# Softmax division as diagonal matrices: two attention stages of a long one-core kernel

## The chip, the cores and the metric

The kernel runs on one core of a Trainium2 chip. One launch computes two transformer blocks of two layers each, all in 32-bit floats. The metric is the time of one execution on the device, in microseconds (us). The kernel before has run three times: 2238.98, 2239.80 and 2239.84 us, median 2239.8 us.

The engines are named as in the profile: PE is the matmul engine (TensorE), PEld its loading of stationary operands (weights), DVE the vector engine, ACT the scalar engine, POOL GpSimd, and SP the queue that issues most DMAs.

## The reference, cut to what matters

Two places of the reference are touched. The first is the dilated window attention of the first block (16 heads, 256 tokens, three dilation groups whose softmax is joint):

```python
p = jnp.exp(s - mx[..., None])
den = jnp.sum(p, axis=-1)
num = jnp.einsum('bdnqhk,bdnkhe->bdnqhe', p, vb.astype(jnp.float32))
...
o = (num / den[..., None]).astype(h.dtype).reshape(B, S, D_MODEL)   # after the groups are joined
```

The second is the differential attention in both layers of the second block (4 heads, two score maps for each head):

```python
p = jax.nn.softmax(jnp.where(mask, s, -jnp.inf), axis=-1)
a = p[:, :, 0] - lam * p[:, :, 1]
return jnp.einsum('bhqk,bkhe->bqhe', a.astype(v.dtype), v)
```

The rest (projections, norms, a convolution mixer, two squared-ReLU MLPs, retention, gated linear attention, routing and 32 experts for each layer) is the same before and after.

## The kernel before, in words

The order on each engine is written out by hand, and semaphores tie the engines together. Weights of about 2 MB a slab pass through a ring of six slots; SP loads a slab when PE has reported a slot free.

**Stage A, the dilated attention** (64 to 344 us of the profile). A loop over c = 0..7 handles two heads at a time. In each round PE makes six projections (`project`, line 1997) of the round's heads and, between them, the attention of the round before. An attention unit is one (head, half of the queries), u = 0..3; u and u+1 make a pair, so there are 16 pairs in all. For each unit:

- PE computes the scores (line 2020), DVE adds the mask and takes the maximum (line 1314), ACT computes the exponential into `att_s`, 128 queries by 512 keys, and its row sum (line 758).
- DVE takes the reciprocal of the sum (line 1323) and multiplies `att_s` by it in place, 128x512 (`scale_prob`, line 1324), and signals `prob_scaled`.
- PE turns `att_s` in four pieces of 128x128 with `te.transpose` against the identity matrix (`turn_p`, line 2030), so that keys lie on the partitions. ACT copies the result out of PSUM (line 766), and one projection later PE multiplies with the values (line 2040).

A pair's eight transposes stand together on PE, after a projection, in the first half of a round and in the second. In the last round the place of the projections is taken by parts of the output product (line 2050).

**Stage D, the differential attention** (around 1018 to 1053 us in layer 0, 1674 to 1709 us in layer 1). Eight units u = (head, half of the queries) for each layer, again in pairs. For each unit ACT makes two exponentials of 128x256, one for each map (line 859). DVE (`d_join`, lines 1503 to 1506) takes two reciprocals, scales map 0 in place, folds lambda into the second reciprocal (a 128x1 operation) and adds the scaled map 1 onto map 0. PE then turns the one joined map, two pieces of 128x128 (`d_turn`, line 2265). The pairs (0,1), (2,3), (4,5) and (6,7) stand between projections (lines 2156, 2163), scores (2253), values (2274) and the retention's products (2284, 2295, 2304).

`spread` (line 1910) is a helper that the prediction compares with: an ordinary matmul of 128x128 with `ones` as the stationary and a diagonal matrix as the moving operand. The diagonal is made by DVE at line 1147 as identity times a column of scalars. `spread` writes two matmuls for each call. `piece` of the experts (line 2493) is compared with too; it writes 16 ordinary matmuls with 128 moving columns for each call.

Of the kernel before, what the change touches and what calls it, by code (L numbers as in the profile page):

```python
# [31 lines left out]
P = 128  # L32
# [174 lines left out]
def program(nc, x_d, xp_d, common_d, const_a_d, const_2_d, param_1_d, param_2_d, param_r_d, pos_d,  # L207
# [8 lines left out]
    def sem(name):  # L216
        return enter(nc.semaphore(name))
# [50 lines left out]
    att_t = [take(512).rearrange("p (j q) -> p j q", j=4) for _ in range(2)]  # L268
    turn_a = take(NT * 6 * 16).rearrange("p (r h d) -> p r h d", r=NT, h=6)
# [68 lines left out]
    qd_n = tok_d.rearrange("p (i r n) -> p i r n", i=2, r=NT)  # L338
    gate_t, r_square, r_root = [tok_d[:, 512 * n:512 * n + 512] for n in (1, 2, 3)]
# [68 lines left out]
    def chunks(b, n):  # L408
# [27 lines left out]
    scored, masked, max_ready, prob_ready, prob_scaled, prob_turned, prob_copied, pv_done, o_copied = [  # L436
        sem("a_" + n) for n in (
            "scored", "masked", "max_ready", "prob_ready", "prob_scaled", "prob_turned", "prob_copied",
# [13 lines left out]
    d_gained, d_summed, d_ready, d_side, d_sided, d_scored, d_max, d_exp, d_joined, d_turned, d_copied, d_out = [  # L452
        sem("d_" + n) for n in ("gained", "summed", "ready", "side", "sided", "scored", "max", "exp", "joined",
# [614 lines left out]
    def _(dve):  # L1068
# [197 lines left out]
        if first:  # L1266
# [53 lines left out]
            def scale_prob(c, u):  # L1320
                p = u % 2
                dve.wait_ge(prob_ready, 4 * c + u + 1)
                own.step(ve.reciprocal(small[:, 6 + p:7 + p], small[:, 4 + p:5 + p]))
                ve.tensor_scalar(att_s[p], att_s[p], small[:, 6 + p:7 + p], None, ALU.mult
                                 ).then_inc(prob_scaled, 1)
            dve.wait_ge(const_a_in, 16)
            for c in range(KD + 1):
                for w in range(2):
                    if c < KD:
                        gain_q(c, 2 * w)  # L1330
                        gain_q(c, 2 * w + 1)
                    if c > 0:
                        mask(c - 1, 2 * w)
                        mask(c - 1, 2 * w + 1)
                    if c < KD:
                        root_q(c, w)
                    if c > 0:
                        scale_prob(c - 1, 2 * w)
                        scale_prob(c - 1, 2 * w + 1)
                    if c < KD:  # L1340
                        norm_q(c, w)
# [58 lines left out]
        if second:  # L1400
# [14 lines left out]
            for lay in range(DEPTH):  # L1415
# [84 lines left out]
                def d_join(u):  # L1500
# [3 lines left out]
                    own.inc(ve.tensor_scalar(att_d[p][:, 0, :], att_d[p][:, 0, :], small[:, 40:41], None, ALU.mult))  # L1504
                    own.step(ve.tensor_scalar(small[:, 42:43], small[:, 41:42], small[:, 28:29], None, ALU.mult))
                    ve.scalar_tensor_tensor(out=att_d[p][:, 0, :], in0=att_d[p][:, 1, :], scalar=small[:, 42:43],
                                            in1=att_d[p][:, 0, :], op0=ALU.mult, op1=ALU.add).then_inc(d_joined, 1)
# [61 lines left out]
                d_join(0)  # L1569
                d_join(1)  # L1570
# [3 lines left out]
                d_join(2)  # L1574
                d_join(3)
                d_mask(4)
                d_mask(5)
                d_join(4)
                d_join(5)
# [3 lines left out]
                d_join(6)  # L1583
                d_join(7)
# [292 lines left out]
    def _(pe):  # L1877
# [106 lines left out]
        if first:  # L1984
# [39 lines left out]
            def turn_p(c, u):  # L2024
                n = 4 * c + u
                pe.wait_ge(prob_scaled, n + 1)
                if n >= 2:
                    pe.wait_ge(prob_copied, n - 1)
                for j in range(4):
                    e = te.transpose(bank(3 + u % 2)[:, P * j:P * j + P], att_s[u % 2][:, P * j:P * j + P], com("ident"))  # L2030
# [96 lines left out]
        if second:  # L2127
# [12 lines left out]
            for lay in range(DEPTH):  # L2140
# [117 lines left out]
                def d_turn(u):  # L2258
                    pe.wait_ge(d_joined, lay * 8 + (u + 1))
# [472 lines left out]
```

## Time and profile before

| | |
|---|---|
| median of three runs | 2239.8 us |
| the profiled execution, its own time | 2239.8 us |
| its span, first to last instruction | 2238.0 us |
| PE busy | 2136.5 us, 95% of the span |
| PEld busy | 1348.7 us, 60% |
| DVE busy | 876.9 us, 39% |
| ACT busy | 343.1 us, 15% |
| chain of waits, by engine | PE 76%, DMA 19%, DVE 2%, issue 1%, ACT 1% |

The times of all instructions come from one execution, read by the hardware profiler. Matmuls are pipelined: the profile gives each a duration of its own that reaches over the next one's start, so what a run of matmuls costs is read from the distance between starts in the timeline, not from the mean duration. The two columns that end a line of a group are the busy time with the mean of one, and the idle time of the engine just before the group with what ended it.

### The profile page before, as it was taken

Reading aid. Unit: us, or ns where it says so; the run is one execution under the profiler, and the core shown is the slowest. Engines: PE = TensorE matmul, PEld = TensorE weight load, DVE = VectorE, ACT = ScalarE, POOL = GpSimd, SP = SyncE. Lnnn points to the kernel's source line nnn. Section 1 sums busy time; section 2 is a strip of 40 time slices with the busy share of each in tenths; the row PEclk is TensorE's granted clock in tenths of the full one; section 3 lists DMA queues with packets and bytes.
Section 4 is the critical chain, followed back from the end, with each engine's and each line's share of the span. In section 5 each row is a group of like instructions: output and inputs, shape, how many; then the busy total and the mean of one; then the engine's idle time right before and its main releaser. Section 6 shows DMA issues by size and latency. Waiting matters only on the chain.

```text
span 2238.0 us, 25518 instructions
## 1 busy us (share of the span) xinstructions
PE 2136.5 (95%) x10046; PEld 1348.7 (60%) x10046; DVE 876.9 (39%) x1937; ACT 343.1 (15%) x657; POOL 21.5 (1%) x28
## 2 busy tenths in 40 slices
PE   9999999999999999999999989888999999889888
PEld 5666668888888888757644443343657554333333
DVE  3444433455331455465443222222355643222222
ACT  1222221000000000224111101010323111100110
POOL 0000000000000000000000000000000000000000
PEclk9999999999999999999999999999999999999999
DMA  7333346787445686423399999999632599999996
GB/s 312 113 130 125 132 151 241 264 303 267 142 151 221 254 309 246 143 102 132 157 369 411 429 429 428 429 428 417 236 122 76 229 401 421 428 429 428 429 428 279
DMA packets 108582, 623.22 MB, mean 278 GB/s; under 512 B 6096, under 2 KB 8528, under 8 KB 73424
## 3 DMA queue, kind: packets, MB, share of 16 engines
q1 hardware_dynamic: 94816, 566.63, 63.0%
q0 software_dynamic: 12672, 50.33, 6.1%
q10 hardware_dynamic: 1008, 5.07, 0.6%
q8 instruction: 59, 0.97, 0.2%
q14 instruction: 27, 0.22, 0.0%
HBM read 620.96 MB, written 1.05 MB: 278 GB/s over the span
## 4 chain that ended last, share of the span: by engine, by line
PE 76%; DMA 19%; DVE 2%; issue 1%; ACT 1%; SPq 0%; DVEq 0%; ACTq 0%
DMA ring<-in_w_up 18%; PE ps L1922 15%; PE ps L2480 14%; PE ps L1997 11%; PE ps L1959 10%; PE ps L2163 5%; PE ps L2514 4%; PE ps L2156 3%; PE ps L2313 2%; PE ps L2452 2%; PE ps L2493 1%; PE ps L2050 1%; PE ps L2020 1%; PE ps L2040 1%; PE ps L2030 1%
## 5 line engine op out<-in xcount | busy, mean ns | idle before, releaser
L2480 PE MATMUL ps<-ring,hT 128*64 128x512 f32 x1984 | 460.8, 619 | 67.9 <-DMA ring<-in_w_up 52.5
L2480 PEld LDWEIGHTS ps<-ring,hT 128*64 128x64 f32 x1984 | 166.7, 142 | 352.1 <-issue 345.6
L1922 PE MATMUL ps<-hT,ring 128*128 128x256 f32 x1408 | 309.8, 381 | 3.6 <-ACT tmp L690 2.4
L1922 PEld LDWEIGHTS ps<-hT,ring 128*128 128x128 f32 x1408 | 267.9, 191 | 41.9 <-issue 3.1
L1997 PE MATMUL ps<-ring,hT 128*128 128x384 f32 x768 | 256.4, 487 | 1.9 <-DMA ring<-in_a_wqkv 1.8
L2514 PE MATMUL ps<-ring,arena 128*64 128x512 f32 x1024 | 226.8, 595 | 1.4 <-ACT arena L995 1.4
L1959 PE MATMUL ps<-arena,ring 128*128 128x256 f32 x1024 | 224.5, 378 | 0.0
L1959 PEld LDWEIGHTS ps<-arena,ring 128*128 128x128 f32 x1024 | 193.3, 189 | 28.1
L1997 PEld LDWEIGHTS ps<-ring,hT 128*128 128x128 f32 x768 | 142.2, 190 | 93.2 <-DMA ring<-in_a_wqkv 2.5
L2514 PEld LDWEIGHTS ps<-ring,arena 128*64 128x64 f32 x1024 | 70.6, 137 | 139.8 <-issue 138.0
L1219 DVE SCALAR_TENSOR_TENSOR arena<-arena,small 128x512 f32<-128x512 f32 x168 | 126.4, 752 | 6.0
L2452 PE MATMUL ps<-arena 128*128 128x256 f32 x512 | 124.0, 385 | 2.0 <-DVE arena L1751 2.0
L2452 PEld LDWEIGHTS ps<-arena 128*128 128x128 f32 x512 | 91.9, 189 | 36.9 <-issue 26.4
L2163 PE MATMUL ps<-ring,hT 128*128 128x512 f32 (+1 forms) x320 | 113.9, 511 | 0.0
L1733 DVE RECIPROCAL arena<-arena 128x512 f32<-128x512 f32 x32 | 107.3, 3354 | 1.1
L1732 DVE TENSOR_SCALAR arena<-arena 128x512 f32<-128x512 f32 x32 | 13.7, 429 | 220.1 <-ACT arena L988 220.1
L1738 DVE TENSOR_TENSOR arena<-arena,ps 128x512 f32<-128x512 f32 x32 | 34.5, 1080 | 145.4 <-PE ps L2480 145.4
L1751 DVE COPY arena<-ps 128x512 f32<-128x512 f32 x32 | 22.2, 692 | 170.0 <-PE ps L2514 170.0
L2163 PEld LDWEIGHTS ps<-ring,hT 128*128 128x128 f32 x320 | 59.5, 190 | 46.4 <-issue 42.5
L1212 DVE TENSOR_TENSOR arena<-tmp 128x1024 f32<-128x1024 f32 x16 | 19.6, 1227 | 169.9 <-ACT tmp L690 169.9
L983 ACT ACTIVATE hT<-arena 128x512 f32 x60 | 38.1, 636 | 272.3 <-PE ps L2480 261.6
L1286 DVE TENSOR_TENSOR arena<-ps,arena 128x384 f32<-128x384 f32 x32 | 17.8, 556 | 144.7 <-ACT arena L738 144.7
(380 smaller groups left out, 1756.6 us busy)
## 6 DMA issues: line engine op xcount, KB each, us to landing
ring<-in_w_gate SPq DMA_DIRECT2D x44, 2048.0 KB, 17.1
ring<-in_w_up SPq DMA_DIRECT2D x44, 2048.0 KB, 17.3
ring<-in_w_down SPq DMA_DIRECT2D x44, 2048.0 KB, 15.9
ring<-in_mlp_w SPq DMA_DIRECT2D x32, 2048.0 KB, 8.0
arena<-in_w_mod POOLq DMA_DIRECT2D x24, 2048.0 KB, 9.7
ring<-in_w_up SPq DMA_DIRECT2D x40, 1024.0 KB, 9.0
ring<-in_w_down SPq DMA_DIRECT2D x40, 1024.0 KB, 8.9
ring<-in_a_wqkv SPq DMA_DIRECT2D x24, 1536.0 KB, 6.8
```

What stands on the lines that cost most here:

```text
L983: e = sc.activation(xg.rearrange("p (k s) -> p k s", k=KD)[:, :, SB * m:SB * m + SB], src, ACT.Copy)
L1219: e = ve.scalar_tensor_tensor(out=mod_acc, in0=w[:, k, :], scalar=small[:, 16 + k:17 + k], in1=mod_acc, op0=ALU.mult, op1=ALU.add)
L1733: own.step(ve.reciprocal(eb, eb))
L1922: e = te.matmul(out[:, j, :], w[:, k, c0 + 128 * j:c0 + 128 * j + 128], src[:, k, :], start=(k == order[0]), stop=(k == order[-1]))
L1959: e = te.matmul(chunks(0, 8)[:, o, :], w[:, k, 128 * o:128 * o + 128], u3[j % 3][:, k, :], start=(start and k == 0 and o % 2 == 0), stop=F ...
L1997: e = te.matmul(bank(r)[:, 0:WIDTH_A], h3[:, k, r * P:(r + 1) * P], weights[:, k, :], start=(k == HEAD_ORDER[0]), stop=(k == HEAD_ORDER[-1]))
L2156: e = te.matmul(out[:, j, :], w[:, k, c0 + P * j:c0 + P * j + P], h3[:, k, :], start=(k == SUM_ORDER[0]), stop=(k == SUM_ORDER[-1]))
L2163: e = te.matmul(out, h3[:, k, r * P:(r + 1) * P], w[:, k, c0:c0 + width], start=(k == 0), stop=(k == KD - 1))
L2313: e = te.matmul(out_2(o), w[:, k, P * (o % 4):P * (o % 4) + P], src, start=(start and k == ks[0] and o % 2 == 0), stop=False, skip_group_c ...
L2452: e = te.matmul(chunks(0, 8)[:, k, :], ysb[:, k * P:(k + 1) * P], selT, start=False, stop=False, skip_group_check=True)
L2480: e = te.matmul(bank(b)[SB * h:SB * h + SB], xg[:, P * k + SB * h:P * k + SB * h + SB], slabs.tile(n + h).rearrange("p (k n) -> p k n", k= ...
L2514: e = te.matmul(bank(6 + o)[SB * h:SB * h + SB], ueT[:, P * k + SB * h:P * k + SB * h + SB], slabs.tile(n + h).rearrange("p (k n) -> p k n ...
```

## The change: what it does

Both stages no longer divide the probabilities on DVE. Instead DVE makes a 128x128 diagonal matrix (the identity times a column of scalars) for each divisor, and PE multiplies the undivided probabilities with that matrix, in place of the transpose. For a block X of queries by keys and a diagonal D, the matmul with X stationary and D moving gives the transposed X with each query's column scaled.

- Stage A: `scale_prob` becomes `diagonal`; the 128x512 operation becomes one of 128x128. `turn_p` keeps four instructions for each unit, now `te.matmul` with `den_diag`.
- Stage D: `d_join` becomes `d_diagonal`: a 128x128 diagonal for map 0, and one for map 1 that holds minus lambda over its sum. `d_turn` issues four matmuls for each unit where two transposes stood: the two maps are added in PSUM (`start` on map 0, `stop` on map 1).
- Two new 128x128 tiles hold the diagonals of stage A; those of stage D lie in `tok_d`. Two semaphores are renamed. No wait is added or taken away.

```diff
-            def scale_prob(c, u):
+            def diagonal(c, u):
                 p = u % 2
                 dve.wait_ge(prob_ready, 4 * c + u + 1)
                 own.step(ve.reciprocal(small[:, 6 + p:7 + p], small[:, 4 + p:5 + p]))
-                ve.tensor_scalar(att_s[p], att_s[p], small[:, 6 + p:7 + p], None, ALU.mult
-                                 ).then_inc(prob_scaled, 1)
+                ve.tensor_scalar(den_diag[p], com("ident"), small[:, 6 + p:7 + p], None, ALU.mult
+                                 ).then_inc(diag_ready, 1)
...
-                def d_join(u):
+                def d_diagonal(u):
                     p = u % 2
                     dve.wait_ge(d_exp, lay * 8 + (u + 1))
                     own.step(ve.reciprocal(small[:, 40:42], small[:, 36 + 2 * p:38 + 2 * p]))
-                    own.inc(ve.tensor_scalar(att_d[p][:, 0, :], att_d[p][:, 0, :], small[:, 40:41], None, ALU.mult))
+                    own.inc(ve.tensor_scalar(den_d[2 * p], com("ident"), small[:, 40:41], None, ALU.mult))
                     own.step(ve.tensor_scalar(small[:, 42:43], small[:, 41:42], small[:, 28:29], None, ALU.mult))
-                    ve.scalar_tensor_tensor(out=att_d[p][:, 0, :], in0=att_d[p][:, 1, :], scalar=small[:, 42:43],
-                                            in1=att_d[p][:, 0, :], op0=ALU.mult, op1=ALU.add).then_inc(d_joined, 1)
+                    ve.tensor_scalar(den_d[2 * p + 1], com("ident"), small[:, 42:43], None, ALU.mult
+                                     ).then_inc(d_diag, 1)
...
             def turn_p(c, u):
...
                 for j in range(4):
-                    e = te.transpose(bank(3 + u % 2)[:, P * j:P * j + P], att_s[u % 2][:, P * j:P * j + P], com("ident"))
+                    e = te.matmul(bank(3 + u % 2)[:, P * j:P * j + P], att_s[u % 2][:, P * j:P * j + P],
+                                  den_diag[u % 2], start=True, stop=True)
...
                 def d_turn(u):
...
                     for k in range(NT):
-                        e = te.transpose(bank((2, 7)[u % 2])[:, k * P:(k + 1) * P], att_d[u % 2][:, 0, k * P:(k + 1) * P],
-                                         com("ident"))
+                        for w in range(2):
+                            e = te.matmul(bank((2, 7)[u % 2])[:, k * P:(k + 1) * P], att_d[u % 2][:, w, k * P:(k + 1) * P],
+                                          den_d[2 * (u % 2) + w], start=(w == 0), stop=(w == 1))
                     e.then_inc(d_turned, 1)
```

In stage A the order on PE stays as it was. Before, around the first pair of a round (x8 counts the instructions that the code writes):

```order
L1997 MATMUL ps<-ring,hT 128x384 x8
L2030 MATMUL ps<-common,arena 128x128 x8
L1997 MATMUL ps<-ring,hT 128x384 x8
L2040 MATMUL ps<-arena 64x128 x8
L2020 MATMUL ps<-arena 128x256 x2
```

The same place now, with the changed kernel's line numbers (`project` is 1999, `turn_p` 2032):

```order
L1999 MATMUL ps<-ring,hT 128x384 x8
L2032 MATMUL ps<-arena 128x128 x8
L1999 MATMUL ps<-ring,hT 128x384 x8
L2043 MATMUL ps<-arena 64x128 x8
L2022 MATMUL ps<-arena 128x256 x2
```

Nothing moved; the eight instructions of a pair read the diagonal (in `arena`) where they read the identity (in `common`).

In stage D, PE from the scores of head 2 on, before (2265 is `d_turn`):

```order
L2253 MATMUL ps<-arena 128x256 x4
L2163 MATMUL ps<-ring,hT 128x256 x8
L2265 MATMUL ps<-common,arena 128x128 x4
L2253 MATMUL ps<-arena 128x256 x4
L2163 MATMUL ps<-ring,hT 128x256 x8
L2274 MATMUL ps<-arena 128x256 x2
```

The same place now (2269 is `d_turn`):

```order
L2256 MATMUL ps<-arena 128x256 x4
L2166 MATMUL ps<-ring,hT 128x256 x8
L2269 MATMUL ps<-arena 128x128 x8
L2256 MATMUL ps<-arena 128x256 x4
L2166 MATMUL ps<-ring,hT 128x256 x8
L2278 MATMUL ps<-arena 128x256 x2
```

A pair has eight written instructions where it had four; their place among the others is the same.

## Rows read from the trace of the kernel before

**Rows 1.** Windows view: stretch, busy by engine (instructions), PE clock, DMA share, GB/s.
```profile
64.00:344.00 280.00, 279.33 (x1350) 179.48 (x1350) 122.02 (x424) 78.11 (x176) 0.00 (x0) 1.00 0.35 126
```

**Rows 2.** Chain of waits, 64 to 344 us, shares by line.
```profile
by line: PE ps L1997 73.0%; PE ps L2040 5.9%; PE ps L2020 5.8%; PE ps L2050 5.8%; PE ps L2030 5.3%; PE ps L2007 4.1%; ACT arena L751 0.2%; issue 0.1%
```

**Rows 3.** Timeline, PE, stage A, two pairs: start us, length us, instructions.
```profile
104.58 1.19 PE L2030 MATMUL ps<-common,arena 128*128 128x128 f32 x8
105.60 5.33 PE L1997 MATMUL ps<-ring,hT 128*128 128x384 f32 x16
...
118.50 1.04 PE L2030 MATMUL ps<-common,arena 128*128 128x128 f32 x8
119.38 0.49 PE L2007 MATMUL ps<-common,arena 128*128 128x128 f32 x3
```

**Rows 4.** Timeline, PE, `spread` called twice.
```profile
613.06 0.61 PE L1910 MATMUL ps<-rstd,common 128*128 128x128 f32 x4
613.50 0.61 PE L1910 MATMUL ps<-arena,common 128*128 128x128 f32 x4
613.95 2.32 PE L1922 MATMUL ps<-hT,ring 128*128 128x256 f32 x10
```

**Rows 5.** Timeline, PE, one call of `piece` and what follows.
```profile
1123.82 3.84 PE L2493 MATMUL ps<-tmp,arena 128*128 128x128 f32 x32
1127.49 0.60 PE L2501 MATMUL ps<-common,arena 128*128 128x128 f32 x4
```

**Rows 6.** Waits view, stage A, weight loads: us in total, times, longest us.
```profile
PEld ps L2030 <- DVE arena L1324: 3.6, 13, 0.4
```

**Rows 7.** Groups by form, DVE: count, busy us, mean ns, idle before.
```profile
L1324 DVE TENSOR_SCALAR arena<-arena,small 128x512 f32<-128x512 f32 x32 | 15.6, 487 | 1.1
L1147 DVE TENSOR_SCALAR rstd<-common,tok 128x128 f32<-128x128 f32 x10 | 2.4, 283 | 0.2
L1504 DVE TENSOR_SCALAR arena<-arena,small 128x256 f32<-128x256 f32 x16 | 5.7, 355 | 0.6
```

**Rows 8.** Timeline, PE, stage D of layer 0, three of its four pairs.
```profile
1028.04 0.60 PE L2265 MATMUL ps<-common,arena 128*128 128x128 f32 x4
1028.57 1.13 PE L2253 MATMUL ps<-arena 64*128 64x256 f32 x8
...
1039.96 3.72 PE L2163 MATMUL ps<-ring,hT 128*128 128x256 f32 x16
1043.78 0.44 PE L2265 MATMUL ps<-common,arena 128*128 128x128 f32 x2
1044.90 0.44 PE L2265 MATMUL ps<-common,arena 128*128 128x128 f32 x2 [0.68 <-DVE arena L1506]
1045.27 1.14 PE L2253 MATMUL ps<-arena 64*128 64x256 f32 x8
1046.33 3.72 PE L2163 MATMUL ps<-ring,hT 128*128 128x256 f32 x16
1049.89 1.03 PE L2274 MATMUL ps<-arena 128*128 128x256 f32 x4
...
1051.92 0.66 PE L2265 MATMUL ps<-common,arena 128*128 128x128 f32 x4
1052.41 1.03 PE L2274 MATMUL ps<-arena 128*128 128x256 f32 x4
```

**Rows 9.** Timeline, DVE, unit 5 of layer 0: the join.
```profile
1044.36 0.48 DVE L1506 SCALAR_TENSOR_TENSOR arena<-arena,small 128x256 f32<-128x256 f32 x1
```

**Rows 10.** Timeline, ACT, the end of unit 5's exponential.
```profile
1043.43 0.19 ACT L859 ACTIVATION_READ_ACCUMULATOR arena<-arena,small 128x1 f32 x1
```

**Rows 11.** Timeline, PEld, the output product after stage D, layer 0.
```profile
1065.26 6.77 PEld L2313 LDWEIGHTS ps<-hT,ring 128*128 128x128 f32 x32 [1.43 <-DVE hT L1478]
```

**Rows 12.** Windows view, start of the experts of layer 0 (columns as above).
```profile
1110.00:1120.00 10.00, 10.00 (x48) 3.38 (x50) 7.65 (x22) 0.60 (x1) 0.00 (x0) 1.00 0.14 57
1140.00:1200.00 60.00, 60.00 (x314) 28.86 (x312) 20.57 (x41) 9.35 (x19) 0.00 (x0) 1.00 0.99 409
```

More of the change, by code:

```diff
@@ L268, in program @@
     att_t = [take(512).rearrange("p (j q) -> p j q", j=4) for _ in range(2)]
+    den_diag = [take(P) for _ in range(2)]
     turn_a = take(NT * 6 * 16).rearrange("p (r h d) -> p r h d", r=NT, h=6)
@@ L338, in program @@
     qd_n = tok_d.rearrange("p (i r n) -> p i r n", i=2, r=NT)
+    den_d = [tok_d[:, P * n:P * n + P] for n in range(4)]
     gate_t, r_square, r_root = [tok_d[:, 512 * n:512 * n + 512] for n in (1, 2, 3)]
@@ L435, in program @@
         "half_done", "unit_read", "q_gained", "q_summed", "q_ready", "q_turned", "q_copied")]
-    scored, masked, max_ready, prob_ready, prob_scaled, prob_turned, prob_copied, pv_done, o_copied = [
+    scored, masked, max_ready, prob_ready, diag_ready, prob_turned, prob_copied, pv_done, o_copied = [
         sem("a_" + n) for n in (
-            "scored", "masked", "max_ready", "prob_ready", "prob_scaled", "prob_turned", "prob_copied",
+            "scored", "masked", "max_ready", "prob_ready", "diag_ready", "prob_turned", "prob_copied",
             "pv_done", "o_copied")]
@@ L451, in program @@
         "product", "ready", "scored", "decayed", "used")]
-    d_gained, d_summed, d_ready, d_side, d_sided, d_scored, d_max, d_exp, d_joined, d_turned, d_copied, d_out = [
-        sem("d_" + n) for n in ("gained", "summed", "ready", "side", "sided", "scored", "max", "exp", "joined",
+    d_gained, d_summed, d_ready, d_side, d_sided, d_scored, d_max, d_exp, d_diag, d_turned, d_copied, d_out = [
+        sem("d_" + n) for n in ("gained", "summed", "ready", "side", "sided", "scored", "max", "exp", "diag",
                                 "turned", "copied", "out")]
@@ L1337, in _ @@
                     if c > 0:
-                        scale_prob(c - 1, 2 * w)
-                        scale_prob(c - 1, 2 * w + 1)
+                        diagonal(c - 1, 2 * w)
+                        diagonal(c - 1, 2 * w + 1)
                     if c < KD:
@@ L1568, in _ @@
                 dve.wait_ge(d_sided, lay * 4 + 4)
-                d_join(0)
-                d_join(1)
+                d_diagonal(0)
+                d_diagonal(1)
                 d_mask(2)
@@ L1573, in _ @@
                 rope_r(0)
-                d_join(2)
-                d_join(3)
+                d_diagonal(2)
+                d_diagonal(3)
                 d_mask(4)
                 d_mask(5)
-                d_join(4)
-                d_join(5)
+                d_diagonal(4)
+                d_diagonal(5)
                 rope_r(1)
@@ L1582, in _ @@
                 d_mask(7)
-                d_join(6)
-                d_join(7)
+                d_diagonal(6)
+                d_diagonal(7)
                 decayed(0)
@@ L2025, in turn_p @@
                 n = 4 * c + u
-                pe.wait_ge(prob_scaled, n + 1)
+                pe.wait_ge(diag_ready, n + 1)
                 if n >= 2:
@@ L2258, in d_turn @@
                 def d_turn(u):
-                    pe.wait_ge(d_joined, lay * 8 + (u + 1))
+                    pe.wait_ge(d_diag, lay * 8 + (u + 1))
                     if u >= 2:
```

## The prediction

> **What bounds the kernel now.** I read the windows view of stage A first. PE is busy 279.33 of 280.00 us at a granted clock of 1.00, the upper of its two levels, while DVE has 122 us of work and ACT 78 [rows 1]. The chain of waits says the same: every step of the stretch but 0.3% is a PE line, and the turned probabilities (line 2030) are 5.3% of it [rows 2]. So in stage A a nanosecond on PE is a nanosecond of the kernel, and DVE time is worth only what PE waits for it. The waits view gives that: the weight loads of line 2030 wait 3.6 us in all for DVE's line 1324, 13 times [rows 6], most of it under matmuls that still run. What reaches the matmuls is seen in the timeline, from the start of a pair to the next group's start. In the second half of a round a pair takes 119.38 - 118.50 = 0.88 us; in the first half 105.60 - 104.58 = 1.02 us [rows 3]. The pair without a stall is 8 transposes at 0.109 to 0.110 us. The other loses 0.14 us between its two units, because DVE scales the second block too late. Seven rounds have such a first half; the eighth, under the output product, I take to be without the stall.
>
> **What one instruction costs.** The change swaps a transpose for an ordinary matmul of the same shape, 128x128 stationary and 128 moving columns, 32-bit. The number of instructions in the code does not settle this; the number of recorded ones does. A pair of stage A writes 8 transposes and the timeline has x8 [rows 3]. `spread`, the same kind of matmul as the new one (a diagonal made by DVE is moving), writes 2 for each call and the timeline has x4 [rows 4]. `piece` writes 16 and has x32 [rows 5]. So each ordinary 32-bit matmul goes through PE twice and a transpose once. One pass costs (613.95 - 613.06) / 8 = 0.111 us [rows 4] and, with a restart in it, (1127.49 - 1123.82) / 32 = 0.115 us [rows 5]. I take 0.112 us a pass: an ordinary matmul is 0.224 us, against 0.109 for the transpose. The first distance after PE has stood still is longer: 3.67 - 31 x 0.1115 = 0.21 us for `piece` [rows 5], about 0.10 more than a pass.
>
> The Trainium skill, page "TensorE: Matmul & The Clock Gate", section Terms, speaks harder against this change: the transpose mode of trn2 is four times faster for FP32. The trace has 0.224 to 0.109, a ratio of 2.05, so the page's ratio does not hold for these rows; what it would give stands with the third rival.
>
> **Stage A, PE.** 32 units in 16 pairs. A pair was 8 records and becomes 8 matmuls, 16 records: 16 x 0.112 = 1.79 us. The nine pairs without a stall gain 1.79 - 0.88 = 0.91 us each, 8.2 us. The seven with a stall gain 1.79 - 1.02 = 0.77 us each, 5.4 us, since the stall goes: PE needs the second unit only after 8 passes of the first, 0.90 us later instead of 0.44, and DVE has it earlier too. Sum 13.6 us, all of it on the path.
>
> **Stage A, DVE.** Line 1324 goes from 487 ns (128x512) to a 128x128 multiplication of the identity, 283 ns in line 1147 [rows 7]: 32 x 0.204 = 6.5 us less. None of it counts beyond the 7 x 0.14 = 1.0 us of stall that the sum above already takes away. ACT's copy of a turned unit starts up to 0.91 us later, but a whole projection of 5.3 us lies between it and the matmul that reads it [rows 3]. No DVE or ACT step comes late by this.
>
> **Stage D, PE.** For each unit 2 transposes become 4 matmuls, 8 records; a pair goes from 4 records to 16.
>
> - Pair (0,1): now 1028.57 - 1028.04 = 0.53 us, of which 4 x 0.109 = 0.44 are passes and 0.09 is the change to the next group's shape, which stays [rows 8]. After: 1.79 + 0.09 = 1.88 us, so +1.35 us. Pair (2,3) has the same four records and the same +1.35.
> - Pair (6,7): now 1052.41 - 1051.92 = 0.49 us [rows 8], with a short restart. After: 1.79 + 0.10 = 1.89 us, so +1.40 us.
> - Pair (4,5) is the one place where DVE covers the work. The projection of 16 ahead of it would let go at 1039.96 + (1049.89 - 1046.33) = 1043.52, but unit 4 starts at 1043.78 and unit 5 at 1044.90, after an idle 0.68, and the next group at 1045.27 [rows 8]. On DVE the two big operations of a unit go from 355 and 486 ns (line 1504 and the join) to 283 each [rows 7, 9], 0.27 us less. Unit 4 is then ready at about 1043.51, just when PE is. Its 8 passes with a restart need 8 x 0.112 + 0.10 = 1.00 us, to 1044.52. Unit 5 cannot begin its reciprocal before its exponential ends at 1043.62 [rows 10]; the join ended at 1044.84 [rows 9], and of the 0.27 us the exponential leaves some 0.23. It is ready at 1044.61, and PE starts it at about 1044.66. Its 8 passes, a restart and the change of shape take 0.90 + 0.10 + 0.09, to 1045.75. That is +0.48 us, with 0.9 us of the work in the old waits. Were nothing covered it would be +1.35 us, were all of it covered 0.
>
> A layer gains 1.35 + 1.35 + 0.48 + 1.40 = 4.58 us, two layers 9.2 us. DVE loses 16 x 0.27 = 4.4 us of work in stage D, worth nothing beyond pair (4,5).
>
> **Does it arrive at the end?** After stage D the norms wait for the values that PE makes, and PE waits 1.43 us for them at 1065.26 [rows 11]: that chain starts with PE's last values, so it moves with them. The experts later are bound by weights: the DMA engines are 0.99 busy from 1140 to 1200 us. But from 1110 to 1120 they are at 0.14 [rows 12]: the slots are full and the stream restarts only when PE frees one. A late PE therefore starts the stream late by the same amount, and nothing is absorbed. The granted clock is 1.00 already [rows 1, 12], so nothing is to be won or lost there.
>
> **Sum.** 13.6 + 9.2 = +22.8 us on the profiled execution's own 2239.8 us, which is also the median of the runs shown: 2262.6 us, 1.0% slower.
>
> **Rivals.**
>
> 1. The second record isn't a second pass for this matmul, so that it costs 0.112 us. For: the code of stage A has as many instructions as before. Then stage A is 9 x (0.90 - 0.88) + 7 x (0.90 - 1.02) = -0.7 us; in stage D a pair has 8 records, 0.90 us: +0.46, +0.46, +0.51, and pair (4,5) about +0.04, so 1.5 a layer. In all +2.3 us: 2242.1 us, no change that can be told. Against it stand x4 for two and x32 for sixteen [rows 4, 5]. Chance 3%.
> 2. The other side: PE has room, and the DVE work is what counts. The place is the wait ahead of a pair, the price of a pair on PE is 0.91 us, and DVE decides only where PE now waits longer than that. If it did everywhere, the 6.5 + 4.4 us of DVE would come back: 2228.9 us, faster. Only pair (4,5), with 1.0 us of waiting, passes that point; stage A's 0.14 us does not [rows 3, 8]. Chance 1%.
> 3. Each new pass shows its weight load: its stationary block changes every time and only 128 columns cover it, so that a pass costs the restart's 0.21 us. Stage A: a pair 3.41 us, 7 x 2.39 + 9 x 2.53 = 39.5 us; stage D 3.0 + 3.0 + 3.0 + 1.8 = 10.7 a layer. In all +61 us: 2300.7 us. Against it: `piece` changes its stationary block each time too, and 32 records need 3.67 us [rows 5]. Chance 3%. The skill's factor of four makes a matmul 0.436 us, a pair of stage A 3.49 us and a sum of +62.9 us, 2302.7 us; it would come out here, and this 3% is for both.
> 4. The experts' stream absorbs what stage D adds, because it is the bound there [rows 12]; stage A's part stays: 2239.8 + 13.6 = 2253.4 us. Against it the 0.14 of DMA share before it. Chance 5%.
>
> **How the numbers follow.** The forecast has 88%. Its own range is 2259 to 2266: below, a pass of 0.110 instead of 0.112 takes 384 x 0.002 = 0.8 us off and a better cover in pair (4,5) up to 1.0; above, 0.115 adds 1.2 us, pairs (4,5) without cover 1.7, and the two together with small new waits some 3.4. The runs shown lie within 0.9 us of each other. To hold 8 in 10 with some of the fourth rival I give 2257 to 2268. What a measurement here can tell from no change is about 0.2%, 4.5 us: slower by more holds the forecast and rivals 3 and 4, 96%; within it rival 1, 3%; faster rival 2, 1%.
>
> **What would show it.** In the changed profile: x256 records of `turn_p` and x128 of `d_turn`; the distance from a pair's start to the next group 1.79 us in both halves of a round, the stall between units gone; DVE's diagonal at 283 ns; in stage D 1.9 us for three pairs and about 2.2 from PE's arrival for (4,5); the same DMA-bound stretch, moved by about 18 us in layer 0 and 23 in layer 1. I am wrong if the pairs have x8, if passes lie 0.2 us apart, or if the experts' stretch ends less late than it begins.

## The result, and the profile after

The changed kernel takes 2253.98 us, the median of four runs (2249.54 to 2255.23); the kernel before took 2239.82 us in four runs beside it (2238.98 to 2240.95). The ratio is 1.0064, with a 95% interval from 1.0053 to 1.0077: 14.3 us slower, 11.9 to 17.2. The prediction said slower, with 2262.6 us and a range down to 2257. The direction was right; the time lies 3 us below that range, and some 8 us of the forecast loss did not arrive.

The profiled execution of the changed kernel took 2256.0 us, its span 2254.2 us.

**Stage A** is where the time goes. The windows view over its 292.2 us (columns as in [rows 1]) shows the same full PE, and less DVE work:

```profile
69.80:362.00 292.20, 291.53 (x1472) 194.49 (x1472) 115.08 (x420) 80.25 (x175) 0.00 (x0) 1.00 0.33 120
```

The timeline of PE at the two pairs of [rows 3] (fences of this document leave rows out where `...` stands):

```profile
111.45 1.95 PE L2032 MATMUL ps<-arena 128*128 128x128 f32 x16
113.23 5.33 PE L1999 MATMUL ps<-ring,hT 128*128 128x384 f32 x16
...
126.14 1.95 PE L2032 MATMUL ps<-arena 128*128 128x128 f32 x16
127.92 0.49 PE L2009 MATMUL ps<-common,arena 128*128 128x128 f32 x3
```

A pair has x16 records where it had x8, and both halves of a round take the same 1.78 us (113.23 - 111.45, 127.92 - 126.14): the stall in the first is gone. The groups by form (`turn_p`, `d_turn` and the diagonal of stage A) and the waits view of the stage agree. Of the old 3.6 us of waiting [rows 6], 1.1 us in six waits are left:

```profile
L2032 PE MATMUL ps<-arena 128*128 128x128 f32 x256 | 31.2, 275 | 0.0
L2269 PE MATMUL ps<-arena 128*128 128x128 f32 x128 | 16.4, 279 | 0.0
L1326 DVE TENSOR_SCALAR arena<-common,small 128x128 f32<-128x128 f32 x32 | 9.2, 287 | 1.1
```
```profile
PEld ps L2032 <- DVE arena L1326: 1.1, 6, 0.2
```

**Stage D** of layer 0, PE, all four pairs; it answers to [rows 8]:

```profile
1045.14 1.94 PE L2269 MATMUL ps<-arena 128*128 128x128 f32 x16
1047.02 1.13 PE L2256 MATMUL ps<-arena 64*128 64x256 f32 x8
...
1055.95 1.94 PE L2269 MATMUL ps<-arena 128*128 128x128 f32 x16
1057.73 1.03 PE L2278 MATMUL ps<-arena 128*128 128x256 f32 x4
...
1063.32 2.28 PE L2269 MATMUL ps<-arena 128*128 128x128 f32 x16
1065.53 1.14 PE L2256 MATMUL ps<-arena 64*128 64x256 f32 x8
...
1072.18 2.05 PE L2269 MATMUL ps<-arena 128*128 128x128 f32 x16
1074.07 1.03 PE L2278 MATMUL ps<-arena 128*128 128x256 f32 x4
```

The distances from a pair to the next group are 1.88, 1.78, 2.21 and 1.89 us.

**Where it comes back.** The table sets the start of the same instruction in both traces against each other. A lasting change of the delay is time lost or won between two rows. (Delays are taken from unrounded times.)

| place on PE | before, us | after, us | delay |
|---|---|---|---|
| first `turn_q` (line 2007, now 2009) | 37.36 | 42.50 | 5.14 |
| last pair of stage A, group behind it | 339.36 | 358.11 | 18.74 |
| the sums after it | 389.31 | 406.39 | 17.08 |
| stage D, layer 0, behind the last pair | 1052.41 | 1074.07 | 21.65 |
| experts' loop, layer 0 | 1266.48 | 1287.18 | 20.70 |
| `permute` for layer 1 (line 2137, now 2140) | 1546.86 | 1564.70 | 17.83 |
| turns of the last expert pair | 1564.85 | 1581.35 | 16.50 |
| stage D, layer 1, behind the last pair | 1708.33 | 1729.39 | 21.06 |
| experts' loop, layer 1 | 1922.41 | 1942.49 | 20.08 |
| gates of the last expert pair (line 2480, now 2484) | 2203.02 | 2220.92 | 17.89 |
| end of the span | 2238.0 | 2254.2 | 16.2 |

Stage A adds 13.60 us, stage D 4.57 us in layer 0 (over 17.08) and 4.56 us in layer 1 (over 16.50). Then some 4 us go again at the end of each layer, at the one place where PE's program has an `If`. After the experts' loop stands `pe.If(more_blocks(pe) > 0)` for further blocks of routed tokens; here PE takes the `Else` and goes on with `permute`, or in layer 1 with the last expert pair. PE before, at that place in layer 0 and in layer 1 (a number in brackets is the idle time ahead of the group and what ended it):

```profile
1536.60 7.09 PE L2514 MATMUL ps<-ring,arena 128*64 128x512 f32 x32
1546.86 1.93 PE L2137 MATMUL ps<-arena 128*128 128x16 f32 x16 [3.18 <-issue]
...
2203.02 1.60 PE L2480 MATMUL ps<-ring,hT 128*64 128x512 f32 x6 [3.44 <-issue]
```

And after:

```profile
1557.27 7.09 PE L2518 MATMUL ps<-ring,arena 128*64 128x512 f32 x32
1564.70 1.93 PE L2140 MATMUL ps<-arena 128*128 128x16 f32 x16 [0.34 <-PE ps L2518]
...
2220.92 1.51 PE L2484 MATMUL ps<-ring,hT 128*64 128x512 f32 x6 [1.27 <-ACTq L1064]
```

"issue" means that nothing which the profile shows was waited for. The 3.18 us become 0.34, the 3.44 us 1.27: 2.84 and 2.17 us. The rest of the two fours is PE's clock. In before, the stretch shortly behind the gap runs at the lower of its two levels, 1.2 GHz; in after the same place runs at 2.4 GHz. (Such a stretch is called half-clock below; in the windows its PE clock is 0.50, or a value between where it fills a part.) Windows of before (the gap of layer 0, the stretch behind it, the stretch behind the gap of layer 1):

```profile
1543.70:1546.80 3.10, 0.00 (x0) 0.00 (x0) 0.85 (x2) 0.60 (x1) 0.00 (x0) 1.00 1.02 420
1549.00:1552.40 3.40, 2.77 (x8) 0.92 (x10) 0.48 (x2) 0.00 (x0) 0.00 (x0) 0.51 1.01 417
2204.30:2207.70 3.40, 3.40 (x10) 1.19 (x8) 0.00 (x0) 0.00 (x0) 0.00 (x0) 0.50 1.01 417
```

And of after, in layer 0 (2222.0 to 2225.4 us, in layer 1, has 1.00 too):

```profile
1567.40:1570.80 3.40, 3.34 (x16) 1.20 (x18) 0.00 (x0) 0.00 (x0) 0.00 (x0) 1.00 1.02 422
```

That takes another 1.33 us (17.83 to 16.50) and 1.69 us (17.89 to 16.20). In all 4.17 and 3.86 us, 8.0 us in these two profiles (the recorded expectations add the rounded parts and say 8.1).

The trace also has the branch instruction itself, on PE's sequencer (durations in ns, least, median and greatest of the two layers; then their starts). Before, and below it after:

```profile
L2581 PEldq COMPARE_BRANCH  x2: 5922/5993/6064, 1540.5 to 2196.2; - x2
```
```profile
L2585 PEldq COMPARE_BRANCH  x2: 333/340/347, 1561.2 to 2216.3; - x2
```

The sequencer reaches the branch while matmuls still wait ahead of PE. In before it stays in it for 5.9 and 6.1 us, so that the queued matmuls run out and PE stands still; in after it is through in a third of a microsecond.

What the branch waits for is PE's own code, as I read it. The profile lists instruction traffic as a queue of its own; the section on queues, before and then after (packets, MB, share):

```profile
q8 instruction: 59, 0.97, 0.2%
```
```profile
q8 instruction: 60, 0.98, 0.2%
```

0.97 MB in 59 packets is 16 KB a packet. In before such a packet begins at 1543.91, 0.8 us after the start of the last matmul of line 2514 (1543.10), and PE goes on 3 us later. In after the packet of this place begins at 1564.84, when `permute` has already started at 1564.70. The Trainium skill, page "Perfetto Trace Analysis", section "The 4-stage abstract model", says that an instruction has 64 bytes; a packet would then be 256 instructions, by my estimate from that figure. No row here shows an instruction's size, but the packet counts of the runs below agree with 256: 59 packets in the kernels with 0, 8 or 192 PE instructions more than before, 60 with 256 or 448, 62 with 768.

The change makes PE's code longer. In the records a written transpose is one record of a weight load and one of a matmul, two instructions; a written 32-bit matmul is twice that, four. Stage A's 128 written ones add 256 instructions, exactly one block; stage D adds 96 in a layer, 32 matmuls at four instead of 16 transposes at two. At the branch of layer 0 the whole change has moved the code by 352, at that of layer 1 by 448 (the trace of after has 448 more instructions, 25966 against 25518).

The remaining differences in the table belong to single executions: the 5.1 us at the start are half-clock stretches, discussed with `before_again`, and the 1.7 us after stage A are a stretch at 0.66 in before (374 to 379 us) that after has not. About 1 us goes in each layer between stage D and the experts' loop (21.65 to 20.70, 21.06 to 20.08), and I leave it open; in layer 0 it goes between 1189 and 1266 us, where the second profile of the same kernel shifts by 0.2 us against before and the other profiles by -1.6 to +1.8.

### The profile page after: what moved, and what is told of

Same layout as the page of the kernel before. It is cut to its first block, busy times and chain, and to the rows that moved or that the text cites. A ratio compares the mean times of both kernels' runs of the same rounds, so it can differ in the third digit from the quotient of the medians.

```text
span 2254.2 us, 25966 instructions
## 1 busy us (share of the span) xinstructions
PE 2160.2 (96%) x10270; PEld 1368.6 (61%) x10270; DVE 866.7 (38%) x1937; ACT 346.8 (15%) x657; POOL 21.5 (1%) x28
## 4 chain that ended last, share of the span: by engine, by line
PE 77%; DMA 19%; DVE 2%; ACT 1%; issue 1%; SPq 0%; DVEq 0%; ACTq 0%
DMA ring<-in_w_up 18%; PE ps L1924 15%; PE ps L2484 14%; PE ps L1999 11%; PE ps L1961 10%; PE ps L2166 5%; PE ps L2518 4%; PE ps L2159 3%; PE ps L2317 2%; PE ps L2456 2%; PE ps L2497 1%; PE ps L2032 1%; PE ps L2053 1%; PE ps L2022 1%; PE ps L2043 1%; PE ps L2269 1%
## 5 line engine op out<-in xcount | busy, mean ns | idle before, releaser
L2484 PEld LDWEIGHTS ps<-ring,hT 128*64 128x64 f32 x1984 | 157.6, 141 | 354.0 <-issue 349.9
```

The lines of the kernel that those rows point to most:

```text
L2484: e = te.matmul(bank(b)[SB * h:SB * h + SB], xg[:, P * k + SB * h:P * k + SB * h + SB], slabs.tile(n + h).rearrange("p (k n) -> p k n", k= ...
```

## The experiments

The landmarks in the traces serve as the measure; "delay" is always against the profile of before. The theory (theory 1 of the expectations): the local costs are as forecast, and some 8 us come back at the two branches because the code was moved. Its rivals: one of the two stages costs less than its distances say, or the experts' weight stream absorbs stage D's part.

**`a_only`: stage A's half of the change alone, `d_only`: stage D's.**

```diff
+    den_diag = [take(P) for _ in range(2)]
-                ve.tensor_scalar(att_s[p], att_s[p], small[:, 6 + p:7 + p], None, ALU.mult
+                ve.tensor_scalar(den_diag[p], com("ident"), small[:, 6 + p:7 + p], None, ALU.mult
-                    e = te.transpose(..., com("ident"))          # turn_p
+                    e = te.matmul(..., den_diag[u % 2], start=True, stop=True)
```

> Stage A's part of the change alone. Every theory agrees on the local cost: 16 pairs of 16 records, +13.6 us over stage A. They differ on what comes back later. Theory 1 (code place): PE's code after the experts' loop is read from memory in blocks of 16 KB, and whether PE stands still after the jump there depends on where the target lies in a block. The 128 additional records are 256 PE instructions, weight load and matmul, which at 64 bytes each is one whole block: the phase is that of the kernel before, so the gap of about 3.2 us before line 2137 stays and nothing is given back: about 2253 us. Theory 2 (the experts' weight stream absorbs what a stage adds before it): only stage D's share can be absorbed, so again about 2253. Theory 3 (PE's additional work in A is hidden somewhere): below 2249.

> Stage D's part of the change alone, +4.58 us in each layer before the experts. Theory 1 (code place): the target of the jump after the experts' loop moves by 96 instructions in layer 0 and by 192 in layer 1 within its 16 KB block, as in the whole change; the gap falls from 3.2 to about 0.3 us and the half-clock window that follows it goes, 4.2 us in layer 0 and some 3.9 in layer 1. With about 1 us a layer from the weight stream, 2239.8 + 9.2 - 8.1 - 1.9 = 2239.0 us, no change. Theory 2 (the stream absorbs): about 2239.8 to 2240, and then the delay against the kernel before is already gone while the experts' loop runs, not at its end. Theory 3 (nothing is given back): 2249.

`a_only` took 2253.04 us (2250.90 to 2257.18), ratio 1.0071 [1.0055, 1.0088]; `d_only` 2240.72 us (2238.16 to 2245.09), ratio 1.0006 [0.9996, 1.0016]; the kernel before in the same job 2239.36 us. Stage D's half costs nothing that can be told in sum, though each layer's stage D takes its 4.6 us. `permute` of layer 0 in `a_only`:

```profile
1558.12 3.18 PE L2139 MATMUL ps<-arena 128*128 128x16 f32 x16 [3.35 <-issue]
```

and in `d_only`:

```profile
1553.45 1.93 PE L2138 MATMUL ps<-arena 128*128 128x16 f32 x16 [0.34 <-PE ps L2516]
```

A whole block more in front of the branch leaves the gap; 96 instructions remove it, and in layer 1 the 192 of `d_only` leave 1.27 us instead of 3.44. In `a_only` stage A moves the delay from 1.19 to 14.79 us, 13.60 again. In `d_only` the delay is 9.26 us at the end of stage D and 9.37 us at 1514 us, deep in the weight-bound loop: the stream absorbs nothing in layer 0, and 2.5 us come back behind the loop there. In layer 1 about 3.9 us come back behind the loop and another 2.3 us inside it, where before has six half-clock stretches and `d_only` five.

**The gap and the clock come apart in these two profiles.** `d_only` has no gap in layer 0 and yet a half-clock stretch behind the branch; `a_only` has a gap of 3.34 us in layer 1 and none. Windows of `d_only`, then of `a_only`:

```profile
1557.40:1560.70 3.30, 3.30 (x10) 0.98 (x8) 0.00 (x0) 0.00 (x0) 0.00 (x0) 0.50 1.02 415
```
```profile
2216.00:2222.00 6.00, 6.00 (x30) 2.42 (x28) 0.00 (x0) 0.00 (x0) 0.00 (x0) 1.00 1.02 419
```

Over all thirteen profiles of this document (those of the kernels further below among them), nine have the gaps and four have none. The half-clock stretch behind the branch is there in 16 of the 18 places with a gap and in 2 of the 8 without. From the start of the loop's last group of line 2514 to the turns of the last expert pair, layer 0 takes 28.25 us in before and 29.8 to 30.1 in the other eight with gaps, against 24.08 or 25.77 us without; layer 1 takes 24.3 to 26.2 us against 22.24. The means differ by 4.9 and 3.5 us, 8.3 us in all. So 8 us is an average of two parts: 5 us or a little more of standstill, which every kernel with gaps has at both branches, and about 3 us of clock, which is more often there behind a gap but can come or stay away in a single execution.

**`phase`: the kernel before, its code moved by 96 and 192 instructions without stage A or D being touched.** The warm-up matmuls of `fill` are cut into more and narrower ones, with about the same number of columns.

```diff
-            fill(6, 3)
+            fill(30, 3, 83)                      # 30 of 83 columns for 6 of 416
-                fill(FILL, 4)                    # FILL = 8
+                fill(*((32, 4, 104) if lay else (FILL, 4)))
```

> The kernel before, with nothing of the change. The 6 warm-up matmuls of 416 columns at the start are 30 of 83, and in layer 1 the 8 warm-up matmuls of the routing are 32 of 104: the same columns, 96 PE instructions more by layer 0's jump and 192 by layer 1's. Theory 1: the gap after the experts' loop falls to about 0.3 us in both layers and the clock does not fall behind it: 2239.8 - 4.2 - 3.9 = about 2231.7 us, faster. Theory 2 and theory 3: nothing changes, 2239.8 us.

2236.89 us (2234.72 to 2238.25), ratio 0.9989 [0.9979, 0.9999]. Both gaps are gone, as expected (0.34 us in layer 0, 1.27 us in layer 1; the branch takes 0.35 and 0.33 us, and 4.2 and 3.9 us of delay go). The time missed, because narrow warm-ups are not as short as their columns. Start of the kernel before, and below it of `phase`, both at a granted clock of 1.00:

```profile
3.52 7.42 PE L1884 MATMUL ps<-common 128*128 128x416 f32 x12 [3.52 <-DMA param<-in_param]
...
12.73 3.49 PE L1997 MATMUL ps<-ring,hT 128*128 128x384 f32 x10 [1.78 <-DMA ring<-in_a_wqkv]
```
```profile
3.48 13.09 PE L1884 MATMUL ps<-common 128*128 128x83 f32 x60 [3.48 <-DMA param<-in_param]
16.37 2.06 PE L1997 MATMUL ps<-ring,hT 128*128 128x384 f32 x3
```

60 records take 12.89 us (16.37 - 3.48), 0.215 us for 83 columns, where 12 of 416 took 7.42 in all. The first projection starts 3.6 us late, and the narrower warm-ups of layer 1 cost 0.5 us: 8.0 - 4.1 = 3.9 us would be left, and 2.5 us (0.2 to 4.7) were measured.

**`after_back`: the changed kernel, its code moved on to whole blocks (512 and 768 instructions), so that the gaps should return.**

```diff
-            fill(6, 3)
+            fill(30, 3, 83)
-                fill(FILL, 4)
+                fill(*((48, 4, 69) if lay else (24, 4, 139)))
```

> The changed kernel with more and narrower warm-up matmuls (same columns), so that layer 0's jump lies 512 and layer 1's 768 PE instructions behind the kernel before, whole 16 KB blocks. Theory 1: the gap of 3.2 us is back in both layers, with the half-clock window: about 8 us slower than the changed kernel, near 2262. Theory 2 and 3: the same as the changed kernel, 2254.

2270.69 us (2270.32 to 2271.27), ratio to before 1.0145 [1.0128, 1.0162]. The gap is back (3.47 us in layer 0, 3.34 in layer 1). It overshot the expected time by the same fault as `phase`: its first projection starts at 16.40 us against 13.27 in after, 3.1 us, and the 48 warm-ups of 69 columns in layer 1 cost about 4.0 us: 2254.0 + 8.0 + 3.1 + 4.0 = 2269.1 us. These 96 records in its timeline:

```profile
1780.59 10.83 PE L1886 MATMUL ps<-common 128*128 128x69 f32 x96
1791.26 0.38 PE L2435 MATMUL ps<-arena 128*128 128x64 f32 x2
```

That is 0.111 us a record ((1791.26 - 1780.59) / 96), what 128 columns cost in [rows 4].

**`phase_skip`: 96 instructions more, but placed in the branch that PE does not take.**

```diff
                 with pe.If(more_blocks(pe) > 0):
+                    for _ in range(24):
+                        te.matmul(bank(4)[:, 0:1], zeros, com("ones")[:, 0:1], start=False, stop=False,
+                                  skip_group_check=True)
```

> The kernel before, with 24 matmuls of one column (96 PE instructions with their weight loads) put into the branch behind the experts' loop that these inputs don't take, in both layers. Nothing more is executed; layer 0's jump stays where it was and its target moves by 96 instructions, layer 1's jump by 96 and its target by 192. Theory 1a (only the target's place in its 16 KB block counts): both gaps fall as they did with the same targets, 2239.4 - 4.2 - 3.9 = about 2231.3 us. Theory 1b (the distance from the jump counts, what was fetched ahead): layer 0's gap stays 3.2 us, layer 1's may stay, 2235 to 2239.4. Theory 2 (code place has no part, the gain in the last such run was the warm-up's): 2239.4.

**`phase_2`: 96 and 192 instructions, added by warm-ups of 104 columns alone.**

```diff
-                fill(FILL, 4)
+                fill(4 * FILL, 4, 104)
```

> The kernel before, with the 8 warm-up matmuls of 416 columns of the routing as 32 of 104 in both layers, and the start as it was. Theory 1: targets 96 and 192 instructions later, gaps gone, -4.2 and -3.9 us, and +0.5 us a layer for the narrower warm-up as it showed in the last such run: 2239.4 - 8.1 + 1.0 = 2232.3 us. Theory 2: 2240.4.

The kernel before in this job took 2239.59 us. `phase_skip` took 2241.41 us (2235.77 to 2244.61), ratio 0.9999 [0.9987, 1.0010], and the gaps stay (3.41 and 3.37 us; the branches take 6.14 and 5.94); `phase_2` took 2231.64 us (2227.51 to 2238.39), ratio 0.9968 [0.9958, 0.9978]. `permute` of layer 0 in `phase_skip` (its first 8 records), then in `phase_2`:

```profile
1548.65 1.51 PE L2137 MATMUL ps<-arena 128*128 128x16 f32 x8 [3.41 <-issue]
```
```profile
1543.55 1.93 PE L2137 MATMUL ps<-arena 128*128 128x16 f32 x16 [0.34 <-PE ps L2514]
```

Both kernels move `permute` by the same number of instructions, and only one loses the gap. So it is not the place of the target in its block that decides, but where the loop and the branch ahead of it lie, or how far the target is from them. `phase_2` is faster than the kernel before and the changed one with nothing but narrower warm-ups: 8.0 us by the medians, 7.2 by the ratio (4.9 to 9.4). Its own profile gives 2.5 us at the branch of layer 0, where a half-clock stretch is left, and 3.9 in layer 1. That the medians come so near to the 8 us is in part luck, since the narrower warm-ups cost some 0.5 us a layer.

**`warm`: a rival for the delay at the start (the half-clock stretches come from PE's idle 1.78 us ahead of the first slab), and `before_again`: the kernel before once more.**

```diff
-            fill(6, 3)
+            fill(8, 3)
```

> The kernel before, with 8 instead of 6 warm-up matmuls at the start. The profiles so far differ by 0 to 7.5 us in when the first attention work is reached, by half-clock windows in the first 31 us. Theory S (PE's idle time before the first slab lets the clock fall): the idle 1.8 us goes, the windows in the first 31 us with it, about 2 us less in the median and a narrower spread. Rival (the windows come whatever PE does in that gap, or by chance in each execution): 2239.4, the same spread. The jump's targets move by 8 instructions only; the gap behind the experts' loop stays at about 3.2 us.

> The kernel before, word for word, for a second profile. If the half-clock windows at the start and at 375 us are a matter of the execution and not of the kernel, they lie elsewhere this time, and the first attention work starts up to 5 us later or not; the gap behind the experts' loop is 3.2 us again in layer 0 and 3.3 in layer 1.

(The expectation calls the rival that the idle time is the cause "theory S".) `warm` took 2238.90 us (2236.95 to 2244.55), ratio 0.9997 [0.9987, 1.0007]. The idle time goes, the first projection is where it was, and the half-clock stretch comes at 22.8 us all the same:

```profile
12.68 3.49 PE L1997 MATMUL ps<-ring,hT 128*128 128x384 f32 x10 [0.48 <-DMA ring<-in_a_wqkv]
```

`before_again` (one run, 2245.09 us) has no edit at all, and yet a half-clock stretch at the start that before did not have. Windows of `before_again` at 20 to 25 us, of after at 25 to 30; before has 1.00 from 20 to 30 us:

```profile
20.00:25.00 5.00, 5.00 (x18) 3.21 (x19) 1.95 (x12) 0.10 (x1) 0.00 (x0) 0.66 1.02 434
```
```profile
25.00:30.00 5.00, 5.00 (x9) 2.58 (x8) 2.15 (x10) 0.49 (x1) 0.00 (x0) 0.50 1.01 430
```

Its first `turn_q` comes 0.9 us late. Among the kernels whose PE code up to there is that of before, that delay is 0.9 (`phase_2`) to 5.1 us (after), and `a_only` has 1.2. The start is thus a matter of the execution; the 5.1 us of after's profile are no part of the change. The gaps at the branches are a matter of the kernel: `before_again` has them as before, 3.46 and 3.45 us.

**`after_whole`: the changed kernel on whole blocks (512 and 768) once more, with warm-ups of 104 columns or wider.**

```diff
-            fill(6, 3)
+            fill(12, 3, 208)
-                    fill(3, 7)                   # and the second fill(3, 7) likewise
+                    fill(9, 7, 139)
-                fill(2, 7)
+                fill(6, 7, 139)
-                fill(FILL, 4)
+                fill(4 * FILL, 4, 104)
```

> The changed kernel with its targets again a whole number of 16 KB blocks behind the kernel before (512 instructions in layer 0, 768 in layer 1), this time by warm-up matmuls of no fewer than 104 columns, since those of 69 and 83 cost about 4 us each time they ran. Theory 1: the gaps are back, +8.1 us on 2254.0, +1 us for the warm-ups: 2263, where the forecast of 2262.6 stood. If the forecast's two sums (13.6 and 9.2 us) were too large, it is nearer 2255.

2264.96 us (2263.52 to 2265.47) beside 2240.52 us, ratio 1.0105 [1.0078, 1.0132]. `permute` of layer 0 (its first 11 records):

```profile
1566.23 2.11 PE L2140 MATMUL ps<-arena 128*128 128x16 f32 x11 [3.25 <-issue]
```

With the gaps back in place the change costs about what was forecast: +24.4 us by the medians, 23.5 by the ratio (17.5 to 29.6), where the sum had +22.8 and the narrower warm-ups may bring about 1 us more (the estimate of the expectation).

**`a_ident` and `a_relief`: the two halves of stage A's change apart.** In `a_ident` PE multiplies with the identity and DVE scales as before; in `a_relief` DVE makes the diagonals and PE transposes as before, so that the division of stage A is left out.

```diff
-                    e = te.transpose(..., com("ident"))                                # a_ident
+                    e = te.matmul(..., com("ident"), start=True, stop=True)
-                ve.tensor_scalar(att_s[p], att_s[p], small[:, 6 + p:7 + p], ...)       # a_relief
+                ve.tensor_scalar(den_diag[p], com("ident"), small[:, 6 + p:7 + p], ...)
```

> The kernel before, with stage A's transposes as ordinary matmuls against the identity, and the division on DVE as it was: the cost of the second pass by itself. In stage A a pair takes 1.79 us in both halves of a round, without a stall between its units, +13.6 us from the first turned query to the end of the values, the same as with DVE relieved. If DVE's relief has a part in it, more. Its place in the code is a whole block later, so the gap behind the experts' loop stays.

> The kernel before, with DVE making the 128x128 diagonal in stage A and PE keeping its transposes: the division in stage A is left out. DVE's relief by itself: the seven pairs of 1.02 us take 0.88, -1.0 us over stage A, and nothing else.

One run each: 2253.27 and 2237.10 us. Over stage A the delay of `a_ident` goes from 1.76 to 15.59, +13.83 us; that of `a_relief` from 1.06 to 0.08, -0.98 us. A pair in the first half of a round in `a_ident`, then in `a_relief`:

```profile
108.06 1.99 PE L2030 MATMUL ps<-common,arena 128*128 128x128 f32 x16
109.89 1.46 PE L1997 MATMUL ps<-ring,hT 128*128 128x384 f32 x4
```
```profile
105.54 1.04 PE L2031 MATMUL ps<-common,arena 128*128 128x128 f32 x8
106.42 0.81 PE L1998 MATMUL ps<-ring,hT 128*128 128x384 f32 x2
```

The second passes are the whole price. DVE's relief is worth 1.0 us alone (a pair goes from 1.02 to 0.88 us). Beside them it is worth 0.2 us in these single profiles (13.83 against 13.60), since the longer first unit already covers most of the stall (1.83 against 1.78 us).

## Why the prediction was right in its steps and wrong in its sum

- **What one instruction costs: right.** x256 and x128 records, 1.78 us for 16 of them, 0.111 us a pass against 0.112. Rival 1 wanted x8 a pair, rival 3 distances of 0.2 us; neither is there.
- **Stage A: right.** 13.6 us forecast, 13.60 measured in the changed kernel and in `a_only`. The stall of seven pairs was there and went (`a_relief`: 0.98 us for 7 x 0.14).
- **Stage A, DVE: right.** 287 ns a diagonal (283 forecast), and nothing that DVE or ACT does comes late. Rival 2 fell with `a_relief`: taking the DVE work away gives 1 us, not 6.5.
- **Stage D: right.** 1.88, 1.78, 2.21 and 1.89 us a pair against 1.88, 1.88, about 2.2 and 1.89 (pair (2,3) is followed by another group than the forecast took, and was 0.10 us shorter before as well); 4.57 and 4.56 us a layer against 4.58. In pair (4,5) unit 5's reciprocal does wait for its exponential, as worked out:

```profile
1063.45 0.17 DVE L1505 RECIPROCAL small<-small 128x2 f32<-128x2 f32 x1 [0.20 <-ACT arena L861]
```

- **"Does it arrive at the end?": this step failed.** It asked of the norms, the experts' weight stream and the clock whether they would give time back, and found that none would. For the stream that was right (`d_only`, 9.26 to 9.37 us). But it took the rest of PE's program to be the same program, later. It is the same instructions at another place in memory, and some 8 us of the time before were a cost of that place, a term that the sum did not have: two standstills of 3.2 and 3.4 us marked "issue", of which 2.84 and 2.17 us went, and the half-clock matmuls behind them, 1.33 and 1.69 us. The forecast looked at the sum of "issue", 1%, among the views and not at where it stood. The statement that nothing was to be won or lost at the clock rested on three windows; the trace of before has 16 half-clock stretches, all outside them, two of them behind these branches.
- **The sum**, with that step mended: 13.6 + 9.1 - 8.0 = +14.7 us, against +14.3 measured (11.9 to 17.2). The agreement is closer than the 8.0 deserves: its clock part differs between single executions by 1.7 us a branch. `after_whole` and `phase_2` show the two parts alone, with the intervals given above: +24.4 us for the change when the gaps stay, -8.0 us for the gaps without the change.
- **The range** was too narrow on its own terms: the terms below the forecast add up to 1.8 us, 2260.8, not the 2259 written, and nothing in it stood for PE's code or for the spread of single executions; the kernel before alone ran from 2236.96 to 2246.83 us in 25 runs of one job, where the forecast knew three within 0.9 us.
- **Rival 4** named 2253.4 us, close to the result, by a mechanism that isn't there. A test by the time alone would have confirmed it; `d_only`'s delay inside the loop of layer 0 refutes it. The changed profile already spoke: I had written that I would be wrong if the experts' stretch ended less late than it began, and so it was, 20.70 us late in the loop and 17.83 right behind it.

**What stays open.** That the time goes inside the branch is in the trace: the branch takes 5.9 to 6.2 us in all nine profiles with gaps and 0.33 to 0.35 us in the four without. That it is the reading of code is an inference from three things that agree: the 16 KB packet that begins while PE's sequencer is in the branch, the silence of every other releaser, and the count. Both gaps are there in all eight profiles with 0, 8, 256, 512 or 768 instructions added ahead of a branch, a whole number of blocks or close to it; both are gone in all four with 96, 192, 352 or 448. `phase_skip` is the thirteenth. Each profile is one execution, but no kernel had the gap at one of its branches and not at the other. Why the code is there in time in some positions and not in others is not settled; `phase_skip` shows that the position of the target alone does not decide. What brings the half-clock stretches, behind the branches and in the loops, is not shown; they come more often behind a gap. What brings the half-clock stretches at the start was not found; idle time of 1.78 us was not it. The 1 us between stage D and the loop is not explained.

## What to carry to other kernels

A 32-bit matmul with a diagonal instead of a transpose would fold a division in for free only where PE waits anyway: in this kernel it doubled PE's time for the step, and with PE full the elementwise work that it saved was worth only the stalls that it ended. Any edit of the code moves everything behind it: before a forecast look for every idle time marked "issue" at a branch and for the duration of the branch instruction, and price them as something the edit may remove or create. When the time comes out well between two theories, compare start times of the same instruction along both traces; the place where the delay jumps names the cause, and an edit that only adds or splits warm-ups tests it alone.

## What the runs showed of the hardware that I had not expected

- A branch behind a loop kept PE's sequencer for 5.9 to 6.2 us in nine profiles, with 3.2 to 3.6 us of standstill on PE, and for 0.33 to 0.35 us in four; in these runs it went by how many instructions stand in the program ahead of it. In 16 of 18 such places, and 2 of 8 without a standstill, a stretch at a granted clock of 0.50 followed the branch.
- Narrow 32-bit matmuls stop getting shorter. Records of 416 columns took 0.36 us (5.75 us for 16), of 104 columns 0.111 (64 in 7.13 us to the next instruction, `phase_2`), of 69 columns 0.111 (`after_back`), no less. With 104 columns the weight loads are busy for 7.13 of the 7.13 us. Where the 16 records of before and the wait behind them took 6.64 us, these take 7.13: 0.5 us a layer that `phase_2`'s gain already bears. The 83-column records at the start took 0.215 us each at the same granted clock, with the weight loads busy for 12.80 of 12.80 us; why these are twice as long was not tested.
- The same kernel shows its half-clock stretches at other places from one execution to the next (before at 374 us, `before_again` at 21 us), and they move the delay of a single profile by some 1 to 5 us.
